# Output projection of a hybrid encoder layer: nine of twelve residual tiles turned by VectorE and ScalarE in place of TensorE

## The reference, cut to what matters

```
x  = x + jnp.concatenate([a, p], axis=-1) @ w_out          # output projection, residual
h2 = rmsnorm(x, norm2_g)
x  = x + jnp.square(jax.nn.relu(h2 @ w_up)) @ w_down       # MLP, d_ff = 4096
```

## Time and profile before

| | us |
|---|---|
| median of 3 runs | 1484.46 (1484.03 to 1484.59) |
| the profiled execution | 1483.54 |
| its span (first to last instruction) | 1481.8 |
| PE busy | 1471.5 (99% of the span) |
| DVE busy | 1042.6 (70%) |
| ACT busy | 705.7 (48%) |
| POOL busy | 401.1 (27%) |

### The profile page before, as it was taken

How to read it: one execution, slowest core, us unless ns; L and a number is a source line. 1 busy time by engine, 2 the same in 40 slices (tenths; PEclk the granted TensorE clock), 3 DMA queues, 4 the chain that set the end, 5 groups by cost and what they waited for, 6 DMA issues and landing times.

```text
span 1481.8 us, 23179 instructions
## 1 busy us (share of the span) xinstructions
PE 1471.5 (99%) x7884; PEld 1312.3 (89%) x7884; DVE 1042.6 (70%) x1301; ACT 705.7 (48%) x1195; POOL 401.1 (27%) x347
## 2 busy tenths in 40 slices
PE   9999999999999999999999999999999999999999
PEld 8999878888888889999999999999888888888887
DVE  6766799999856675544454545448888878878875
ACT  6223399999833344545454545456322322323220
POOL 3467599888910010000000000001320311311300
PEclk9999999999999999999999999999999999999999
DMA  8654331000246639343334323347744343343434
GB/s 262 154 121 112 98 90 24 20 11 14 83 146 250 219 113 413 132 146 125 129 113 157 134 109 134 137 155 291 264 157 153 104 149 122 125 156 105 137 99 183
DMA packets 89066, 209.10 MB, mean 141 GB/s; under 512 B 8240, under 2 KB 27568, under 8 KB 88880
## 3 DMA queue, kind: packets, MB, share of 16 engines
q1 hardware_dynamic: 86816, 197.27, 39.9%
q10 hardware_dynamic: 2192, 11.08, 1.8%
HBM read 129.93 MB, written 71.57 MB: 136 GB/s over the span
## 4 chain that ended last, share of the span: by engine, by line
PE 93%; DVE 2%; ACT 2%; POOL 1%; issue 1%; DMA 0%; ACTq 0%; POOLq 0%; DVEq 0%
PE ps L871 24%; PE ps L873 24%; PE ps L872 24%; PE ps L1134 6%; PE ps L1016 4%; PE ps L1144 3%; PE ps L1031 2%; PE ps L998 2%; PE ps L1032 2%; PE ps L1000 2%; ACT prob L1351 1%; PE ps L1154 1%; POOL prob L2414 0%; DVE pTlo L1744 0%; DVE nmax L1806 0%
## 5 line engine op out<-in xcount | busy, mean ns | idle before, releaser
L871 PE MATMUL ps<-h,wuhi 128*128 128x384 f32 (+1 forms) x904 | 301.5, 334 | 0.2 <-issue 0.2
L873 PE MATMUL ps<-h,wulo 128*128 128x384 f32 (+1 forms) x904 | 301.2, 333 | 0.0
L872 PE MATMUL ps<-h,wuhi 128*128 128x384 f32 (+1 forms) x904 | 301.2, 333 | 0.0
L871 PE MATMUL ps<-wdhi,hidhi 128*128 128x512 f32 x672 | 261.6, 389 | 0.0
L873 PE MATMUL ps<-wdhi,hidlo 128*128 128x512 f32 x672 | 261.6, 389 | 0.0
L872 PE MATMUL ps<-wdlo,hidhi 128*128 128x512 f32 x672 | 261.5, 389 | 0.0
L2220 DVE TENSOR_TENSOR yacc<-yacc,ps 128x1024 f32<-128x1024 f32 x167 | 203.2, 1217 | 78.1 <-PE ps L873 78.1
L1270 ACT ACTIVATE hidhi<-hin 128x1024 fp32r<-128x1024 f32 (+1 forms) x72 | 86.8, 1205 | 300.7 <-PE ps L873 292.8
L2134 DVE TENSOR_TENSOR u<-u,ps 128x384 f32<-128x384 f32 x96 | 53.1, 553 | 181.7 <-PE ps L873 181.7
L871 PEld LDWEIGHTS ps<-h,wuhi 128*128 128x128 f32 x904 | 169.7, 188 | 0.7 <-issue 0.4
L872 PEld LDWEIGHTS ps<-h,wuhi 128*128 128x128 f32 x904 | 169.8, 188 | 0.0
(11 more groups left out here) (217 smaller groups left out, 2804.2 us busy)
## 6 DMA issues: line engine op xcount, KB each, us to landing
hd<-hout SPq DMA_DIRECT2D x64, 384.0 KB, 3.2
hin<-hd SPq DMA_DIRECT2D x48, 512.0 KB, 3.7
hd<-hout SPq DMA_DIRECT2D x32, 576.0 KB, 2.8
hin<-hd SPq DMA_DIRECT2D x24, 768.0 KB, 4.4
wuraw<-in_w_up SPq DMA_DIRECT2D x17, 1024.0 KB, 6.0
wdraw<-in_w_down SPq DMA_DIRECT2D x8, 2048.0 KB, 9.4
h<-h2d ACTq DMA_DIRECT2D x7, 1536.0 KB, 11.6
x2in<-in_x SPq DMA_DIRECT2D x12, 512.0 KB, 3.3
```

Source lines behind the costliest of these rows:

```text
L871: pe.matmul(out, w_hi, m_hi, start=start, stop=False, skip_group_check=resumed)
L872: pe.matmul(out, w_hi, m_lo, start=False, stop=False, skip_group_check=resumed)
L873: return pe.matmul(out, w_lo, m_hi, start=False, stop=stop, skip_group_check=resumed)
```

## The change

TURNED = 9: tiles 0 to 8 are no longer turned by PE. Tiles 9, 10 and 11 still are.

- DVE scales such a tile into PSUM (`junk_banks()`, banks 4 and 5) and then transposes it in 32x32 blocks, `turn_x2(p)`, one instruction 128x1024 from PSUM into `x2turn` in SBUF.
- ACT places the blocks, `place_x2(p)`: 16 copies of 32 partitions x 256 elements from `x2turn` to `x2T[PLACES[p]]`, each to its quarter of the partitions. `h2_bank` gives this array, with a block layout, for tiles below 9.
- ACT writes the throwaway output of the squares into PSUM in place of an SBUF array.
- The order on ACT for p = 1 to 9 becomes `split_c(p+2)`, `square_x2(p)`, `hi_h2(p-1)`, `place_x2(p)`; on DVE `residual(p)`, `split_c(p+2)`, `scale_x2(p)`, `turn_x2(p)`, `lo_h2(p-1)`. `split_c` is one tile further ahead than before.
- On SP `store_h2` comes behind `store_x2` and `load_x2` of its iteration.
- Some semaphores are merged (`rs_out`, `gq_scaled`, `win_edge`, `win_done`, `ms_half`), with the same waits.

```diff
+        TURNED = TT - 3
+        PLACES = (0, 1, 2, 0, 1, 2, 0, 1, 0)
+        def wait_turned(eng, p):
+            if p < TURNED:
+                eng.wait_ge(x2_moved, 16 * p + 16)
+            else:
+                eng.wait_ge(xT2_done, p - TURNED + 1)
+        def x2_block(p, b, r):
+            q = (b + r) % 4
+            return x2T[PLACES[p]][q * 32:q * 32 + 32, b], x2turn[b * 32:b * 32 + 32, q]
+        def junk_banks():
+            return psw[:, 2048:3072]
...
-                if p:
+                if p > TURNED:
                     transpose_x2(p - 1)
...
+            def place_x2(p):
+                wait_place(act, p)
+                for r in range(4):
+                    for b in range(4):
+                        out, src = x2_block(p, b, r)
+                        copy(out, src).then_inc(x2_moved, 1)
...
+            split_c(2)
             square_x2(0)
+            place_x2(0)
             for p in range(1, TT):
-                if p + 1 < TT:
-                    split_c(p + 1)
+                if p <= TURNED:
+                    if p + 2 < TT:
+                        split_c(p + 2)
+                    square_x2(p)
+                    hi_h2(p - 1)
+                    if p < TURNED:
+                        place_x2(p)
+                elif p + 1 < TT:
                     hi_h2(p - 1)
...
             def scale_x2(p):
                 dve.wait_ge(rs2_done, p + 1)
-                if p:
-                    dve.wait_ge(xT2_done, p)
-                dve.scalar_tensor_tensor(xs2[:], x2in[:, p % 2], rsx[:, 0:1], g2b[:], ALU.mult, ALU.mult
-                                         ).then_inc(xs2_done, 1)
+                if p < TURNED:
+                    dve.wait_ge(x2T_done, p)
+                elif p == TURNED:
+                    dve.wait_ge(x2_moved, 16 * TURNED)
+                else:
+                    dve.wait_ge(xT2_done, p - TURNED)
+                dve.scalar_tensor_tensor(junk_banks() if p < TURNED else xs2[:], x2in[:, p % 2], rsx[:, 0:1], g2b[:],
+                                         ALU.mult, ALU.mult).then_inc(xs2_done, 1)
+            def turn_x2(p):
+                dve.wait_ge(xs2_done, p + 1)
+                dve.wait_ge(x2_moved, 16 * p)
+                dve.transpose(x2turn[:], junk_banks().rearrange("p (k q c) -> p q k c", k=KT, q=4)).then_inc(x2T_done, 1)
...
+            split_c(2)
             scale_x2(0)
+            turn_x2(0)
             for p in range(1, TT):
-                if p + 1 < TT:
-                    split_c(p + 1)
-                if p < TT - 2:
+                if p <= TURNED:
+                    residual(p)
+                    if p + 2 < TT:
+                        split_c(p + 2)
+                    scale_x2(p)
+                    if p < TURNED:
+                        turn_x2(p)
                     lo_h2(p - 1)
-                    residual(p)
-                    scale_x2(p)
...
-                if p in (2, 4, 6):
-                    store_h2((p - 2) // 2)
                 store_x2(p)
                 if p + 2 < TT:
                     load_x2(p + 2)
+                if p in (2, 4, 6):
+                    store_h2((p - 2) // 2)
```

More of the change, by code:

```diff
@@ L297, in hybrid_layer @@
         xT2_done = sem("xT2_done")
+        x2T_done = sem("x2T_done")
+        x2_moved = sem("x2_moved")
         x2_half = sem("x2_half")
         ss_half = sem("ss_half")
-        ms_half = sem("ms_half")
         xs2_half = sem("xs2_half")
@@ L486, in wu_place, with blocked, h2_psum, h2_bank @@
             return (wuhi6, wulo6) if isinstance(w, int) and (w, o) == (0, 6) else (wuhi[o], wulo[o])
-        def h2_bank(q, b):
+        TURNED = TT - 3
+        PLACES = (0, 1, 2, 0, 1, 2, 0, 1, 0)
+        def blocked(tile):
+            return tile.rearrange("p k (b t) -> p k b t", b=4)
+        def h2_psum(q, b):
             bank = b - 2 if b > 1 and q == TT // 2 - 1 else 4 + b
             return ps[:, bank].rearrange("p (k c) -> p k c", k=4)
+        def h2_bank(q, b):
+            if 2 * q + b // 2 < TURNED:
+                return x2T[PLACES[2 * q + b // 2]][:].rearrange("p b k t -> p k b t")[:, b % 2 * 4:b % 2 * 4 + 4]
+            return blocked(h2_psum(q, b))
+        def wait_turned(eng, p):
[3 more added lines that the diff above has]
+                eng.wait_ge(xT2_done, p - TURNED + 1)
+        def wait_place(eng, p):
+            last = max((i for i in range(p) if PLACES[i] == PLACES[p]), default=None)
+            eng.wait_ge(x2T_done, p + 1)
+            if last is not None and last % 2:
+                eng.wait_ge(h2_lo, SLOTS * (last // 2 + 1))
+            elif last is not None:
+                eng.wait_ge(h2_sum, 4 * (last // 2 + 1))
+        def x2_block(p, b, r):
[3 more added lines that the diff above has]
+            return psw[:, 2048:3072]
         def h2_staged(q, a):
@@ L498, in h2_half @@
             if q < QT_TILES:
-                return h2_staged(q, 2 * o + low).bitcast(F32R)
-            return h2[1][o][:, low, q - QT_TILES]
+                return blocked(h2_staged(q, 2 * o + low).bitcast(F32R))
+            return blocked(h2[1][o][:, low, q - QT_TILES])
         def h2_full(q, o):
             if q < QT_TILES:
-                return h2_staged(q, 2 * o + 1)
-            return h2raw[o][:, q - QT_TILES]
+                return blocked(h2_staged(q, 2 * o + 1))
+            return blocked(h2raw[o][:, q - QT_TILES])
         def up_bank(par, o):
@@ L1149, in transpose_x2 @@
                 pe.wait_ge(xs2_done, p + 1)
-                if p >= 2:
-                    pe.wait_ge(h2_lo, SLOTS * (p // 2))
                 for k in range(KT):
-                    mm = pe.transpose(h2_bank(p // 2, p % 2 * 2 + k // 4)[:, k % 4], xs2[:, k * P:(k + 1) * P], ident[:])
+                    mm = pe.transpose(h2_psum(p // 2, p % 2 * 2 + k // 4)[:, k % 4], xs2[:, k * P:(k + 1) * P], ident[:])
                 mm.then_inc(xT2_done, 1)
@@ L1160, in transpose_last @@
                 for k in range(4):
-                    mm = pe.transpose(h2_bank(TT // 2 - 1, 2)[:, k], xs2[:, k * P:(k + 1) * P], ident[:])
+                    mm = pe.transpose(h2_psum(TT // 2 - 1, 2)[:, k], xs2[:, k * P:(k + 1) * P], ident[:])
                 mm.then_inc(xT2_half, 1)
@@ L1164, in transpose_last @@
                 for k in range(4):
-                    mm = pe.transpose(h2_bank(TT // 2 - 1, 3)[:, k], xs2[:, (k + 4) * P:(k + 5) * P], ident[:])
+                    mm = pe.transpose(h2_psum(TT // 2 - 1, 3)[:, k], xs2[:, (k + 4) * P:(k + 5) * P], ident[:])
                 mm.then_inc(xT2_done, 1)
@@ L1491, in square_x2 @@
                     act.wait_ge(ss2_done, p)
-                act.activation(junk2[:], x2in[:, p % 2], ACT.Square, scale=D ** -0.5, accum_out=ssx[:]
+                    act.wait_ge(x2T_done, min(p, TURNED))
+                act.activation(junk_banks(), x2in[:, p % 2], ACT.Square, scale=D ** -0.5, accum_out=ssx[:]
                                ).then_inc(ss2_done, 1)
@@ L1499, in square_last @@
                 act.wait_ge(ss2_done, TT - 1)
-                act.activation(junk2[:, 0:512], x2in[:, 1, 0:512], ACT.Square, scale=D ** -0.5, accum_out=ssx[:]
+                act.activation(ps[:, 2], x2in[:, 1, 0:512], ACT.Square, scale=D ** -0.5, accum_out=ssx[:]
                                ).then_inc(ss_half, 1)
                 act.wait_ge(x2_done, TT)
-                act.activation(junk2[:, 512:D], x2in[:, 1, 512:D], ACT.Square, scale=D ** -0.5, accum_out=ssx_b[:]
+                act.activation(ps[:, 3], x2in[:, 1, 512:D], ACT.Square, scale=D ** -0.5, accum_out=ssx_b[:]
                                ).then_inc(ss2_done, 1)
@@ L1706, in _ @@
                     square_last()
[L1707 removed]
+                elif p > TURNED:
                     square_x2(p)
@@ L2324, in norm_x @@
                 rsqrt_mean(rs[:, t:t + 1], msx[:], ssx[:], epsx[:], msx_done, rsx_done, t)
[L2326 to L2333, removed]
             pool.memset(up[:, :, 0:PAD], 0.0)
@@ L2364, in window_step @@
                     ins = pool.tensor_tensor(part, part, edge[:, g, e * PAD:(e + 1) * PAD], ALU.mult)
[L2365 to L2368, removed]
+                ins.then_inc(win_part, 1)
+                pool.wait_ge(win_part, 2 * (s * GROUPS + g) + 1)
+                pool.tensor_scalar(sums, sums, 1.0 / w, 1.0, ALU.mult, ALU.mult).then_inc(win_part, 1)
+                pool.wait_ge(win_part, 2 * (s * GROUPS + g) + 2)
                 c0 = pool_pos(s)
@@ L2552, in _ @@
                 norm_x2(p)
-            norm_halves(1, TT, ms2_done, ss2_done)
+            pool.wait_ge(ss_half, 1)
+            pool.tensor_tensor(msx[:], ssx[:], epsx[:], ALU.add).then_inc(ms2_done, 1)
+            pool.wait_ge(ms2_done, TT)
+            pool.wait_ge(ss2_done, TT)
+            pool.tensor_tensor(msx_b[:], msx[:], ssx_b[:], ALU.add).then_inc(ms2_done, 1)
+            pool.wait_ge(ms2_done, TT + 1)
             pool.wait_ge(xs2_done, TT - 1)
```

28 lines of the change are left out of this document (13 added, 15 removed).

## The result

| | before | after |
|---|---|---|
| median | 1484.31 us | 1515.0 us (1513.95 to 1516.09, 4 runs) |
| ratio | 1 | 1.0207 [1.0195, 1.0219] |
| profiled execution, its span | 1483.54, 1481.8 | 1514.48, 1512.7 |

The account below looks back on a forecast made before the run. PE bounded the kernel before; after, the loop between ACT and DVE delays tile 9's transposes by 7.7 us, plus 1.8 for PE's start from rest: 9.5 us slower, 1494.0 on the median, range 8 in 10 1486 to 1507.

Parts of the forecast that it names:

- The gain on offer, 8.1 us: Output projection, PE: without nine tiles of transposes and without waits, tile 10's transposes start at 527.15 instead of 535.23.
- the loop through `hi_h2`, behind scale and turn: ACT waits for DVE's remainder, then places: 11.65 and 14.68 us per iteration, 26.33 per pair where PE needs 21.78.
- DVE transpose 1.24, 1.17 in a row: DVE, one 128x1024 transpose per tile: 1.24 us long, 1.17 in a row; rival of 2.14 us, chance 0.09.
- 16 copies per tile at 0.30: ACT placing blocks of 32 partitions x 256: 0.30 us each, 4.8 per tile; below 0.25, above 0.40.
- Eight tiles of blocks in the sum: Projection: iteration 1 starts at 432.96 when tile 1 is out; eight iterations, four of each kind, take 105.32 us.
- 7.7: Projection: the transposes of tile 9 can start at 542.9 against 535.2 before, 7.7 us later.
- The waits of PE: PE in the projection: 1.1, 0.8, 3.8, 0.8 us before tiles 7 to 10, 9.4 before tile 9's transposes; 15.8 together.
- the two tiles of lead: Projection: two tiles are rounded in advance, so PE runs ahead and the ACT and DVE loop is hidden in tiles 1 to 6.
- The squares into PSUM, the merged semaphores and the later store, taken at nothing: Other edits cost nothing: squares the same length within 0.05, same waits, and a store nobody needs for two tiles.
- Start from rest, 1.8 us: PE after 9.4 us idle ahead of tile 9's transposes: a slow start costs between 0 and 1.8 us, 1.8 taken.
- The half microsecond for `load_wu`: SP: `load_wu(0)` behind `load_x2(11)` delays square and scale of tile 10 by some half a microsecond, covered by 1.8 us.
- The Trainium skill's rule against the 0.30: ACT blocks: fixed latency exposed between instructions, 0.40 us each, 6.4 per tile; rival of full durations, 1506.8, chance 0.12.

Follow-up runs that it names:

- e2: Changed kernel with four copies of 128 partitions x 256 per tile in place of 16 of 32, so tiles are not turned rightly: 1476.87 us, 0.9945.
- e7: Changed kernel with ACT's and DVE's waits shortened and eight of the 16 blocks placed by POOL, nothing left out: 1476.34 us, 0.9948.
- e5: Changed kernel, same instructions: DVE makes an odd tile's sums before scaling the next, ACT an even tile's extra copy behind the blocks: 1504.75 us, 1.0137.
- e1: Changed kernel with eight forms of placing copy, one per tile (3: four per quarter; 5: 128x256; 6: PSUM source); only trace used, tile 3 row 5.39 us.
- e8: Changed kernel with 46 more matmuls 128x512 on PE, results unused, in its wait for the transposes of tile 9: 1513.39 us, 1.0191.
- e4: Changed kernel with eight of the 16 blocks per tile placed by POOL while ACT places the others, nothing left out: 1485.45 us, 1.0007.

## Why the prediction was wrong, point by point

- *The gain on offer, 8.1 us*: right. e2 and e7 show 7.8 and 8.4.
- *PE bounds, and the loop through `hi_h2`, behind scale and turn, takes its place*: right. Every part but one came as read from rows 4 to 6; the two kinds of iteration measured 13.92 and 16.93, 2.27 and 2.25 over the forecast, of which the blocks are 2.2. e5 changed only the waits and came out at 1504.75 where 1505 was expected.
- *DVE transpose 1.24, 1.17 in a row*: right, 1.25 and 1.18 measured.
- ***ACT: 16 copies per tile at 0.30, the step that failed.*** It measured 0.438. The 0.30 was worked out from copies that all use the same partitions, and it holds for those (e1, tiles 3 and 5); the blocks change the quarter each time, and then the overlap of 0.1 is lost, as well as some 0.02 more. The price was also set too low at its upper end (0.40, the duration without a gap) for the range to hold the time. None of rows 1 to 9 shows two neighbouring copies that change the partitions, but the trace of before has some in the attention stage (timeline of ACT):

```profile
195.09 0.61 ACT L1270 ACTIVATE pThi<-ps 128x512 fp32r<-128x512 f32 x1
195.73 0.63 ACT L1270 ACTIVATE Qs<-QT 64x512 fp32r<-64x512 f32 x1
196.39 0.60 ACT L1270 ACTIVATE pThi<-ps 128x512 fp32r<-128x512 f32 x1
...
198.35 0.62 ACT L1270 ACTIVATE Qs<-QT 64x512 fp32r<-64x512 f32 x1
198.87 1.07 ACT L1270 ACTIVATE pThi<-ps 128x512 fp32r<-128x512 f32 x2
```

By the kernel the first `Qs` is on the partitions 64 to 127: it starts 0.64 after its predecessor and holds its successor up 0.66, both more than a copy lasts. The second is on 0 to 63 and costs 0.52, as usual, though its successor has 128 partitions. So the sign could have been read before the forecast, and in these rows it goes with the first partition of a copy, not with their number. The prediction took only the mean duration of this group (629 ns).
- *Eight tiles of blocks in the sum*: it was nine. I let iteration 1 start when tile 1 was out, and that hid the blocks of tile 0 only because at 4.8 us they would just have ended then; at 7.0 they run over, and iteration 1 started 2.3 us late. With this the sum closes: 9 x 16 x 0.138 = 19.9, on top of 7.7; another 0.85 lay in the trace before the projection began (tile 0 starts at 411.84, not 410.99). Its cause is open: in the traces of the nine experiments, which change next to nothing ahead of this point, tile 0 starts between 411.15 and 413.38. Together this is 28.4 of the measured 28.8.
- *The waits of PE*: forecast 1.1, 0.8, 3.8, 0.8 before tiles 7 to 10 and 9.4 before the transposes; measured from tile 5 on, 18.4 in six waits and 11.3. Since the blocks came dearer, the two tiles of lead were used up two tiles earlier.
- *The squares into PSUM, the merged semaphores and the later store, taken at nothing*: right. The square takes 1.01 us, ACT waits for no store in the projection, and e2 shows the whole gain with them.
- *Start from rest, 1.8 us*: right in kind, 2.1 measured. The half microsecond for `load_wu` that it was to cover shows in e8. After the wait of 11.35 us the granted clock reads 0.67 on average over the next 6.6 us, between its two levels (0.5 and 1.0 in this column), and in e8, without that rest, 1.00. The other starts from rest (5.45 us in place of 3.79 after 3.10 idle) cost nothing in the end, as PE would have waited for the loop all the same: from tile 3 to tile 9 no residual on DVE waits for PE. The Trainium skill, "TensorE: Matmul & The Clock Gate", part 1, says that the idle state is the throttled one and that activity releases it. The trace agrees: the first 24 matmuls took 6.62 us in place of 4.5, and only the next 16 took 3.79 again.
- *The Trainium skill's rule against the 0.30* ("VectorE: DVE Perf Modes", the TRN2 errata): the 0.40 us worked out from its table for a copy of this size agrees with the duration (0.414 here, 0.402 in the wide form), but e1 contradicts that it is exposed between instructions as such: 0.30 between copies on the same partitions. Only where the quarter changes does the next copy wait for the end of the last, and with a source in PSUM as well (tile 6). Of my rivals this one came nearest, 1506.8, by nearly the right size (0.40) for another reason.

## What to carry to other kernels

When work is taken from the engine that bounds, add up the loop of waits through the other engines, not their busy time: here ACT was busy 22 of 31 us per pair, and the loop through it still set the pace. A distance read from rows holds for their shape and for their neighbours: ask of each new instruction whether the one before it starts at the same partition, and look through the whole trace for a pair that is not. And when one engine gets many small pieces, give part of them to one that idles and put whatever others wait for ahead of them; both together were worth 38.7 us here.

## What the runs showed of the hardware that I had not expected

- ACT: two copies 32x256 in a row are 0.30 us apart when both stay in one quarter of the partitions, 0.44 when source or target changes quarter, with a source in PSUM about 0.40 (e1). Before, a copy 64x512 on the partitions 64 to 127 between copies of 128 stands 0.62 to 0.66 from its neighbours, one on 0 to 63 only 0.47 to 0.52.
- POOL: a copy 32x256 across quarters takes 0.45 to 0.80 us (eight in 3.58 to 6.39); while POOL copies, DVE's 128x512 subtractions to fp32r go from 0.69 up to 0.88 (e4, e7), as in these rows of e7:

```profile
473.61 5.72 POOL L2623 COPY x2T<-x2turn 32x256 f32<-32x256 f32 x8 [3.60 <-DVE x2turn L2090]
...
476.44 0.88 DVE L1801 TENSOR_TENSOR stage<-x2T,stage 128x512 fp32r<-128x512 f32 x1
```
- DVE: a transpose 128x1024 of runs of 32 elements from PSUM takes 1.25 us, the 1.24 that was worked out from the 128x640 one, whose source is in SBUF; with single elements apart, from SBUF, 128x1024 takes 2.14. Runs of 32 from SBUF were not measured at this size.
